# A diffusion backbone on one core: the last down projection turned to tokens on partitions, and a fourth buffer of rounded weights

## The chip, the cores and the metric

The kernel runs on one core of one Trainium2 chip. The metric is the device time of one execution in microseconds (us); the time before is the median of three runs, 1262.39 us (1262.36 to 1262.87). TensorE (PE) multiplies and writes to eight PSUM banks of 128 partitions x 512 fp32 values; VectorE (DVE), ScalarE (ACT) and GpSimd (POOL) work on SBUF, the first two also on PSUM; SyncE (SP) issues the loads of weights and the stores of the result.

## What the reference computes

Two layers over 256 latent and 256 context tokens of 1024 channels (P = 128, D = 1024, T = 512): layer 0 has attention, layer 1 a gated DeltaNet, and each ends with a SwiGLU part of hidden width 2816 = 22 x 128 (FT = 22). The change concerns the feed-forward part of layer 1 alone, where only the latent tokens are still needed:

```python
h = modulate(rms_norm(x, norm_g[l, 2]), sh2, sc2)
gate, up = jnp.split(h @ w_gate_up, 2, axis=-1)
y = (jax.nn.silu(gate) * up) @ w_down          # 256 x 2816 times 2816 x 1024
x = x + gt2 * (y * rsqrt(mean(y * y, axis=-1) + 1e-6)) * norm_g[l, 3]
```

`gt2` is a vector of 1024 channels, the same for all tokens; the output is `x` with tokens as rows.

## The kernel before

**Layout.** Activations lie with channels on partitions: `xT[:, k, token]` is channel tile k of 8. A channel's gate (`mods`) is then a value per partition, but a sum over channels, as the norm needs, is a matmul with a matrix of ones, and the output has to be transposed at the end.

**Products in parts.** Weights and activations are fp32 and are each split into a rounded part (fp32r, "hi") and the rest ("lo"). A product is hi x hi + lo x hi + hi x lo. SP loads weight chunks of up to 128 x 1024 values into eight slots `w_raw`; `split_to(n)` on ACT copies chunk n into one of three buffers `w_hi` (L1690), and `split_to(n)` on DVE subtracts that from the raw chunk in place, giving `w_lo` (L1918). ACT may write a `w_hi` buffer only when the products of the chunk three before are done, and `ahead(key)` lets it run two chunks ahead of the product being served.

**The feed-forward part of layer 1.** 44 gate and up chunks `("gate", 1, n)` of 8 contraction tiles, then 24 down chunks `("down", 1, m, part)` of 8, 8 and 6 tiles for each of the 8 output tiles m. `two()` (L1382 to L1394) issues two matmuls for each contraction tile: a weight hi tile is stationary and both parts of the activations move (512 columns, L1392 and L1393), then a weight lo tile and the activations' hi part (256 columns, L1391 and L1394). The first three gate chunks are multiplied together, tile by tile as `pre_norm(3)` delivers `h_both` (`project_lat_together`). Each result holds two halves that ACT copies and DVE adds. `act_both` holds the hidden values' two parts.

**The end.** `take_y` on ACT squares each output tile (L1746) and scales a copy by the gate (L1749), `sum_y` on DVE adds up the squares (L1991), `post_norm(3)` multiplies by ones (L1495), takes Ln and Exp (L1701, L1702), multiplies the 8 tiles by the factor and adds them to `xT` (L1998, L2002). TensorE then transposes `xT` in 16 blocks (L1665), DVE copies four banks of 512 to `out_sb` (L2157), and SP stores two rows of 128 tokens, 512 KB each (L2275).

**Before the feed-forward part.** `project_gdn_out`, `post_norm(2)` and `pre_norm(3)`: ones times the squares of `xT` (L1486), Ln, Exp, then for each channel tile DVE scales (L1958), ACT shifts and rounds (L1723, L1729), DVE takes the rest (L1971).

Each engine follows its own list in program order, held only by semaphores; `take(job, ring)` on TensorE takes the next bank of a ring and waits until its last content was read.

## Time and profile before

| | |
|---|---|
| median of three runs | 1262.39 us |
| profiled execution | 1263.51 us, its span 1261.8 us |
| busy | PE 1182.8 (94%), DVE 625.2, ACT 568.7, POOL 120.6 |
| mean granted TensorE clock | 0.974 |
| latest chain, share of span | PE 81%, DVE 9%, ACT 6% |
| feed-forward part of layer 1 | first matmul at 1053.06, down products from 1183.1 |
| after the last down matmul (starts 1245.09) | 16.7 us to the end of the span |

The span is counted from the first to the last instruction. A matmul's duration in the trace includes the way through the array, so in a dense stream the distance from start to start is the price, not the duration. A clock of 1.00 is 2.4 GHz, 0.50 is 1.2 GHz.

### The profile page before, as it was taken

The page shows a single profiled execution, that of the slowest core. Times are in us where ns is not written, and L with a number is a line of the kernel's source. Part 1 is how long each engine was busy: PE and PEld are TensorE (multiplying, and loading weights), DVE is VectorE, ACT ScalarE, POOL GpSimd, SP SyncE. Part 2 cuts the span into 40 slices and gives each one's busy share as a digit, 9 for nine tenths or more (in the row PEclk, how much of TensorE's full clock was granted, in tenths as well). Part 3 has the DMA queues.
Part 4 walks back from the last instruction along what each step waited for, and adds up shares of the span by engine and source line. Part 5 has one row for each costly group of instructions (what it writes and reads, how often), then busy time and mean ns, then how long its engine had stood idle before and what let it go on. Part 6 is the DMA issues. An engine that isn't in the chain of part 4 may idle for free.

```text
span 1261.8 us, 17880 instructions
## 1 busy us (share of the span) xinstructions
PE 1182.8 (94%) x7085; PEld 923.8 (73%) x7085; DVE 625.2 (50%) x1002; ACT 568.7 (45%) x1071; POOL 120.6 (10%) x116
## 2 busy tenths in 40 slices
PE   6899989989899999999999899999989997999996
PEld 3577734558378888888888558788779875888885
DVE  2532268652543332333222375589976525666554
ACT  2622246753462222223222376775355435665552
POOL 0030320110001111011000000010024100111000
PEclk9899999999999999999999999999979998999998
DMA  9655556642553333333333463234003042666560
GB/s 344 208 163 150 168 197 218 207 114 84 159 141 100 101 100 91 93 96 92 93 99 106 138 150 80 66 89 117 18 20 85 22 131 81 179 189 185 173 178 34
DMA packets 239390, 159.54 MB, mean 126 GB/s; under 512 B 14778, under 2 KB 213836, under 8 KB 239308
## 3 DMA queue, kind: packets, MB, share of 16 engines
q1 hardware_dynamic: 238528, 158.11, 42.5%
q8 instruction: 57, 0.93, 0.3%
q10 hardware_dynamic: 780, 0.29, 0.1%
q14 instruction: 25, 0.20, 0.1%
HBM read 157.33 MB, written 1.05 MB: 126 GB/s over the span
## 4 chain that ended last, share of the span: by engine, by line
PE 81%; DVE 9%; ACT 6%; issue 2%; DMA 1%; SPq 1%; POOL 0%; DVEq 0%; ACTq 0%; POOLq 0%
PE bank L1382 43%; PE bank L1393 9%; PE bank L1394 4%; PE bank L1369 2%; PE bank L1486 2%; PE bank L1436 2%; PE bank L1591 2%; PE bank L1467 1%; PE bank L1601 1%; DVE blocks L1020 1%; DVE outer L1018 1%; ACT h_work L1723 1%; PE bank L778 1%; PE bank L1622 1%; DMA w_raw<-in_ada_w 1%
## 5 line engine op out<-in xcount | busy, mean ns | idle before, releaser
L1382 PE MATMUL bank<-h_both,w_hi 128*128 128x512 f32 x1296 | 404.9, 394 | 2.5 <-issue 2.5
L1918 DVE TENSOR_TENSOR w_lo<-w_raw,w_hi 128x1024 fp32r<-128x1024 f32 (+1 forms) x179 | 220.5, 1234 | 244.3 <-ACT w_hi L1690 243.9
L1382 PEld LDWEIGHTS bank<-h_both,w_hi 128*128 128x128 f32 x1296 | 242.8, 188 | 53.7 <-issue 3.5
L1382 PE MATMUL bank<-h_both,w_lo 128*128 128x512 f32 x648 | 253.1, 391 | 0.0
L1690 ACT ACTIVATE w_hi<-w_raw 128x1024 fp32r<-128x1024 f32 (+1 forms) x179 | 184.0, 1031 | 72.5 <-PE bank L1382 52.9
L1382 PEld LDWEIGHTS bank<-h_both,w_lo 128*128 128x128 f32 x648 | 122.1, 188 | 25.9
L1393 PE MATMUL bank<-h_both,w_hi 128*128 128x512 f32 x308 | 113.0, 405 | 6.2 <-DVE h_both L1971 3.2
L1382 PE MATMUL bank<-act_both,w_hi 128*128 128x512 f32 x352 | 108.4, 389 | 0.0
L2176 POOL TENSOR_TENSOR act_both<-a_tmp,act_both 128x512 fp32r<-128x512 f32 (+1 forms) x44 | 44.7, 1016 | 466.1 <-ACT act_both L1792 283.9
L1394 PE MATMUL bank<-h_both,w_lo 128*128 128x256 f32 x308 | 87.5, 284 | 0.0
L1382 PEld LDWEIGHTS bank<-act_both,w_hi 128*128 128x128 f32 x352 | 66.1, 188 | 13.8
L1393 PEld LDWEIGHTS bank<-h_both,w_hi 128*128 128x128 f32 x308 | 59.3, 192 | 19.7 <-issue 7.1
L1382 PE MATMUL bank<-act_both,w_lo 128*128 128x512 f32 x176 | 68.5, 389 | 0.0
L1394 PEld LDWEIGHTS bank<-h_both,w_lo 128*128 128x128 f32 x308 | 59.4, 193 | 1.8
L1447 PE MATMUL bank<-h_whole,w_raw 128*128 128x256 f32 x256 | 59.1, 385 | 0.7 <-DVE h_whole L1074 0.7
L1393 PE MATMUL bank<-act_both,w_hi 128*128 128x512 f32 x168 | 59.7, 399 | 0.0
L1792 ACT ACTIVATE act_both<-a_tmp 128x512 fp32r<-128x512 f32 x22 | 13.9, 632 | 98.9 <-DVE a_tmp L2028 98.9
L1369 PE MATMUL bank<-w_raw,silu_pad 128*12 128x512 f32 (+2 forms) x384 | 53.0, 605 | 2.6 <-ACT silu_pad L1818 1.3
L1447 PEld LDWEIGHTS bank<-h_whole,w_raw 128*128 128x128 f32 x256 | 48.3, 193 | 7.4 <-issue 1.1
L1991 DVE TENSOR_TENSOR post_acc<-post_acc,post_sq 128x512 f32<-128x512 f32 (+1 forms) x28 | 15.6, 559 | 74.0 <-ACT y L1749 74.0
L1746 ACT ACTIVATE post_sq<-bank 128x512 f32<-128x512 f32 (+1 forms) x24 | 12.7, 527 | 87.5 <-PE bank L1382 67.4
L1857 ACT ACTIVATE probs<-bank,stats 128x256 f32<-128x256 f32 (+1 forms) x64 | 36.6, 579 | 31.0 <-DVE stats L2091 30.9
(283 smaller groups left out, 1693.0 us busy)
## 6 DMA issues: line engine op xcount, KB each, us to landing
w_raw<-in_ada_w SPq DMA_DIRECT2D x96, 512.0 KB, 5.0
w_raw<-in_ffn_w_gate_up SPq DMA_DIRECT2D x88, 512.0 KB, 3.8
w_raw<-in_ffn_w_down SPq DMA_DIRECT2D x32, 512.0 KB, 3.8
w_raw<-in_gdn_w_in SPq DMA_DIRECT2D x32, 512.0 KB, 4.0
w_raw<-in_attn_w_in SPq DMA_DIRECT2D x14, 512.0 KB, 3.9
w_raw<-in_ffn_w_down SPq DMA_DIRECT2D x16, 384.0 KB, 3.4
w_raw<-in_gdn_w_out SPq DMA_DIRECT2D x8, 512.0 KB, 5.2
w_raw<-in_attn_w_in SPq DMA_DIRECT2D x8, 256.0 KB, 3.5
```

The costliest lines, as they stand in the source:

```text
L1369: m = nc.tensor.matmul(banks[0][strip:strip + count, :], silu_pad[:, k, lead:lead + count], w[:, t, :], start=(group == 0 and k < ADA_STRIPS),
L1382: m = nc.tensor.matmul(dst, stationary(a, k), moving(b, k), start=(first and k == kk[0] and a == b == 0), stop=(last and k == kk[-1] and a ...
L1393: nc.tensor.matmul(halves, w(0, k), both, start=start, stop=False)
L1394: return nc.tensor.matmul(dst[:, 0:LAT], w(1, k), both[:, 0], start=False, stop=False)
L1436: m = nc.tensor.matmul(dst, w(a, k)[:, 0:width], (h_hi, h_lo)[b][:, k, lo:T], start=(k == a == b == 0), stop=(k == KT - 1 and a == 1))
L1447: m = nc.tensor.matmul(dst, raw_slot(key)[:, k, :], h_whole[:, k, :], start=(k == 0), stop=(k == KT - 1))
L1486: m = nc.tensor.matmul(dst[:, lo:T], ones, pre_sq[:, k % 4, lo:T], start=(k == 0), stop=(k == KT - 1))
L1591: finish(nc.tensor.matmul(dsts[m][:, 0:keys_of(qb)], q_sb[half, tile, qb * P:(qb + 1) * P], k_sb[half, key_tile(tile), 0:keys_of(qb)], sta ...
L1690: nc.scalar.activation(w_hi[m % N_SPLIT][:, 0:tiles, 0:w], raw_slot(key)[:, 0:tiles, 0:w], ACT.Copy).then_inc(w_hi_ready, 1)
L1857: release(nc.scalar.activation(probs[:, n % PROB_RING, m, 0:keys_of(qb)], bank(("s", n, m))[:, 0:keys_of(qb)], ACT.Exp, bias=stats[:, n % ...
L1918: nc.vector.tensor_tensor(w_lo[where[key] % N_RAW][:, 0:tiles, 0:w], raw_slot(key)[:, 0:tiles, 0:w], w_hi[m % N_SPLIT][:, 0:tiles, 0:w].bi ...
L2176: nc.gpsimd.tensor_tensor(act_lo[:, n // 2, lo:T], a_tmp[:, j % 2, lo:T], act_hi[:, n // 2, lo:T].bitcast(F32), ALU.subtract).then_inc(act ...
```

## The change

The down projection of layer 1 turns its operands round. Its weights are loaded as 22 chunks of two contraction tiles x 512 output channels (`LAST_HALVES`: half 0 or 1 of the channels, then c = 0 to 10). A hidden tile of 128 tokens is stationary (`late_hi`, `late_lo`, 128 x 128) and the weights move, 512 columns at a time, in three matmuls for each contraction tile and each of the two token tiles. The result `("z", half, t)` has tokens on partitions: ACT squares it and sums along the row in the same instruction, and the norm factor is a value per partition. The gate, now a vector along the row, is spread over the partitions by ones x a diagonal matrix that POOL makes (`gate_diag`), in two matmuls (`"row"` jobs). `xT` before the addition is transposed to tokens in four jobs `"xt"` of four blocks, the first before the feed-forward part and the others after gate chunks 10, 12 and 14; ACT copies all six banks to SBUF while it serves gates 4, 5, 6, 12, 14 and 16. DVE multiplies each z by the gate row, and when the factors are there makes each quarter of the output in one instruction, which SP stores as 256 KB.

In this feed-forward part `w_hi` has a fourth buffer, and ACT and DVE split three chunks ahead in place of two, so a buffer waits for the chunk four before it.

The core of the diff; left out are the places in memory, semaphores' names, the ring `"late"` of banks 0, 7 and 1, the removal of the i = 3 branches and of `post_norm(3)` on each engine, the same `hi_slot` and look-ahead in DVE's `split_to`, POOL's writing to `late_lo`, and the old down loop, which stays for layer 0:

```diff
+LAST_HALVES = [(half, c) for half in range(2) for c in range(FT // 2)]
+TOKENS = [(t, half) for t in range(LAT // P) for half in range(2)]
+TURNED_LATE = [("row", 0), ("row", 1), ("xt",) + TOKENS[0], ("xt",) + TOKENS[1], ("xt",) + TOKENS[2], ("xt",) + TOKENS[3]]
...
+    out += [("down", 1, half, c) for half, c in LAST_HALVES]
...
+        y_sums = stats[:, 0, 0:4].rearrange("p (h t) -> p h t", h=2)
+        y_rest, y_scale = stats[:, 1, 0:2], stats[:, 1, 2:4]
...
+        late_hi = at("late_hi", [FT, LAT], F32R, BIG)
+        late_lo = at("late_lo", [FT, LAT], F32R, BIG + FT * LAT * 4)
...
+        w_hi.append(at("w_hi_late", [KT, P], F32R, TAIL))
...
+        LATE = split_no[("gate", 1, 0)]
+        def hi_slot(n):
+            j = n - LATE
+            if j < 0:
+                return n % N_SPLIT
+            return (LATE + j % 4) % N_SPLIT if j % 4 < N_SPLIT else N_SPLIT
+        def hi_before(n):
+            return n - N_SPLIT if n < LATE + N_SPLIT else n - 4 if n > LATE + N_SPLIT else None
         def ahead(key, stop=None):
             last = len(split_chunks) - 1 if stop is None else split_no[stop]
-            return min(split_no[key] + 2, last)
+            return min(split_no[key] + (3 if split_no[key] > LATE else 2), last)
...
+                    if layer and n in LATE_AT:
+                        turn_late(TURNED_LATE[3 + LATE_AT.index(n)])
+                if layer:
+                    down_by_token()
+                    return
...
+            def turn_late(job):
+                dst = take(job, "late")
+                if job[0] == "row":
+                    pe.wait_ge(diag_ready, 1)
+                    m = nc.tensor.matmul(dst, ones, gate_diag[:, 4 * job[1]:4 * job[1] + 4, :], start=True, stop=True)
+                else:
+                    t, half = job[1:]
+                    pe.wait_ge(x_updated, 3 * KT)
+                    for k in range(4):
+                        m = nc.tensor.transpose(dst[:, k * P:(k + 1) * P],
+                                                xT[:, 4 * half + k, CTX + t * P:CTX + (t + 1) * P], ident)
+                finish(m, job)
+            def down_by_token():
+                for half in range(2):
+                    dsts = [take(("z", half, t)) for t in range(LAT // P)]
+                    def add(t, k, w, a, b):
+                        return nc.tensor.matmul(dsts[t], (late_hi, late_lo)[a][:, k, t * P:(t + 1) * P], w[b][:, k % 2, :],
+                                                start=(k == a == b == 0), stop=(k == FT - 1 and a == 1))
+                    for c in range(FT // 2):
+                        key = ("down", 1, half, c)
+                        w = [part.rearrange("p (t a) m -> p t (a m)", t=2) for part in weight_slots(key)]
+                        kk = (2 * c, 2 * c + 1)
+                        if half == 0:
+                            pe.wait_ge(act_hi_ready, FT + kk[1] + 1)
+                            pe.wait_ge(act_lo_ready, FT + kk[1] + 1)
+                        order = [(t, k) for k in kk for t in range(2)] if c < FT // 2 - 1 else [(t, k) for t in range(2) for k in kk]
+                        for t, k in order:
+                            for a, b in ((0, 0), (0, 1), (1, 0)):
+                                m = add(t, k, w, a, b)
+                            if k == FT - 1 and t == 0:
+                                finish(m, ("z", half, 0))
+                        finish(m, key)
+                    done_at[("z", half, 1)] = jobs[0]
...
+                for job in TURNED_LATE[:3]:
+                    turn_late(job)
                 ffn(1)
-                post_norm(3)
-            for half in range(2):
-                for t in range(LAT // P):
-                    dst = take(("out", t, half))
-                    for k in range(4):
-                        pe.wait_ge(x_updated, LAST_SUB * KT + 4 * half + k + 1)
-                        m = nc.tensor.transpose(dst[:, k * P:(k + 1) * P],
-                                                xT[:, 4 * half + k, CTX + t * P:CTX + (t + 1) * P], ident)
-                    finish(m, ("out", t, half))
...
-                    if m >= N_SPLIT:
-                        wait_product(act, split_job(split_chunks[m - N_SPLIT]))
+                    if m >= N_SPLIT and hi_before(m) is not None:
+                        wait_product(act, split_job(split_chunks[hi_before(m)]))
...
-                if i == 3:
-                    nc.scalar.activation(lat_sums[:, m % 2, 0:LAT], src[:, LAT:2 * LAT], ACT.Copy).then_inc(half_out, 1)
-                    wait_evacuated(act, ("y", i, m))
-                    src = lat_sums[:, m % 2]
...
-                if i == 3:
-                    last.then_inc(y_taken, 1)
-                else:
-                    release(last, ("y", i, m))
+                release(last, ("y", i, m))
...
-                    split_to(ahead(key))
+                    split_to(split_no[key] + 3 if layer else ahead(key))
...
-                            nc.scalar.activation(act_hi[:, n // 2, lo:T], a_tmp[:, j % 2, lo:T],
+                            nc.scalar.activation(late_hi[:, n // 2, :], a_tmp[:, j % 2, lo:T],
                                                  ACT.Copy).then_inc(act_hi_ready, 1)
+                        if n in COPIED_AT:
+                            job = TURNED_LATE[COPIED_AT.index(n)]
+                            wait_product(act, job)
+                            dst = gate_row if job[0] == "row" else x_tok[:, job[1], :]
+                            half = job[-1]
+                            release(nc.scalar.activation(dst[:, half * 512:(half + 1) * 512], bank(job), ACT.Copy), job)
...
+                if layer:
+                    square_by_token()
+                    return
...
+            def square_by_token():
+                for half, c in LAST_HALVES:
+                    split_to(ahead(("down", 1, half, c)))
+                    if c < FT // 2 - 1:
+                        continue
+                    for t in range(LAT // P):
+                        wait_product(act, ("z", half, t))
+                        nc.scalar.activation(s_tmp[:, t, :], bank(("z", half, t)), ACT.Square,
+                                             accum_out=y_sums[:, half, t:t + 1]).then_inc(y_squared, 1)
+                        if half:
+                            act.wait_ge(y_bias, 1)
+                            act.wait_ge(y_squared, 3 + t)
+                            link(nc.scalar.activation(y_scale[:, t:t + 1], y_sums[:, 1, t:t + 1], ACT.Ln,
+                                                      bias=y_rest[:, t:t + 1], scale=1.0 / D))
+                            nc.scalar.activation(y_scale[:, t:t + 1], y_scale[:, t:t + 1], ACT.Exp,
+                                                 scale=-0.5).then_inc(y_rstd, 1)
...
-                if i == 3:
-                    dve.wait_ge(half_out, 2 * FT + m + 1)
-                    release(nc.vector.tensor_tensor(lat_sums[:, m % 2, CTX:T], bank(("y", i, m))[:, 0:LAT],
-                                                    lat_sums[:, m % 2, 0:LAT], ALU.add), ("y", i, m))
-                    dve.wait_ge(y_taken, m + 1)
-                else:
-                    wait_evacuated(dve, ("y", i, m))
+                wait_evacuated(dve, ("y", i, m))
...
-                    split_to(ahead(("gate", layer, n)))
+                    split_to(split_no[("gate", layer, n)] + 3 if layer else ahead(("gate", layer, n)))
...
+                if layer:
+                    finish_by_token()
+                    return
...
+            def finish_by_token():
+                rows = lambda ap, half: ap[:, half * 512:(half + 1) * 512]
+                for half, c in LAST_HALVES:
+                    split_to(ahead(("down", 1, half, c)))
+                    if c < FT // 2 - 1:
+                        continue
+                    wait_evacuated(dve, ("row", half))
+                    for t in range(LAT // P):
+                        dve.wait_ge(y_squared, 2 * half + t + 1)
+                        nc.vector.tensor_tensor(rows(y_gated[:, t], half), bank(("z", half, t)), rows(gate_row, half),
+                                                ALU.mult).then_inc(y_gated_ready, 1)
+                    if half == 0:
+                        nc.vector.tensor_scalar(y_rest, y_sums[:, 0, :], 1.0 / D, RMS_EPS, ALU.mult,
+                                                ALU.add).then_inc(y_bias, 1)
+                dve.wait_ge(y_gated_ready, 4)
+                for t, half in TOKENS:
+                    wait_evacuated(dve, ("xt", t, half))
+                    dve.wait_ge(y_rstd, t + 1)
+                    nc.vector.scalar_tensor_tensor(out=rows(out_sb[:, t], half), in0=rows(y_gated[:, t], half),
+                                                   scalar=y_scale[:, t:t + 1], in1=rows(x_tok[:, t], half),
+                                                   op0=ALU.mult, op1=ALU.add).then_inc(out_ready, 1)
...
-                post_norm(3)
-            for half in range(2):
-                for t in range(LAT // P):
-                    job = ("out", t, half)
-                    wait_product(dve, job)
-                    release(nc.vector.tensor_copy(out_sb[:, t, half * 512:(half + 1) * 512], bank(job)), job)
...
+                wait_product(pool, ("y", 2, 0))
+                pool.wait_ge(mods_ready, 8)
+                nc.gpsimd.tensor_tensor(gate_diag, ident.unsqueeze(1).to_broadcast([P, KT, P]),
+                                        mods[:, 1, 5, :, 1:2].to_broadcast([P, KT, P]),
+                                        ALU.mult).then_inc(diag_ready, 1)
...
+                if kind == "down" and key[1]:
+                    return columns(ffn_w_down[1][2 * key[3] * P:2 * (key[3] + 1) * P, :], key[2] * 512, 512)
...
-            for t in range(LAT // P):
-                for half in range(2):
-                    wait_evacuated(sp, ("out", t, half))
-                sp.dma_start(out[0, t * P:(t + 1) * P, :], out_sb[:, t, :]).then_inc(out_stored, 16)
-            sp.wait_ge(out_stored, 16 * (LAT // P))
+            for n, (t, half) in enumerate(TOKENS):
+                sp.wait_ge(out_ready, n + 1)
+                cols = slice(half * 512, (half + 1) * 512)
+                sp.dma_start(out[0, t * P:(t + 1) * P, cols], out_sb[:, t, cols]).then_inc(out_stored, 16)
+            sp.wait_ge(out_stored, 16 * len(TOKENS))
...
+LATE_AT, COPIED_AT = (10, 12, 14), (4, 5, 6, 12, 14, 16)
```

## Rows read from the trace of the kernel before

**Rows 1.** Windows of 20 us: duration, busy (instructions) by engine, clock, DMA, GB/s.
```profile
1060.00:1080.00 20.00, 17.00 (x97) 14.46 (x96) 10.48 (x15) 12.22 (x21) 2.22 (x3) 1.00 0.56 157
...
1200.00:1220.00 20.00, 20.00 (x115) 17.38 (x114) 11.12 (x13) 10.49 (x16) 0.00 (x0) 1.00 0.65 190
```

**Rows 2.** Timeline, PE, around gate chunks 2 to 5: start, duration, what, idle before.
```profile
1063.94 0.39 PE L1392 MATMUL bank<-h_both,w_hi 128*128 128x512 f32 x1
1066.41 0.47 PE L1393 MATMUL bank<-h_both,w_hi 128*128 128x512 f32 x1 [2.08 <-DVE w_lo L1918]
...
1070.34 0.47 PE L1393 MATMUL bank<-h_both,w_hi 128*128 128x512 f32 x1 [0.92 <-DVE w_lo L1918]
...
1073.19 0.40 PE L1393 MATMUL bank<-h_both,w_hi 128*128 128x512 f32 x1
```

**Rows 3.** Timeline, ACT and DVE, the splits of chunks 3 and 4.
```profile
1063.95 1.05 ACT L1690 ACTIVATE w_hi<-w_raw 128x1024 fp32r<-128x1024 f32 x1
...
1067.89 1.04 ACT L1690 ACTIVATE w_hi<-w_raw 128x1024 fp32r<-128x1024 f32 x1
...
1065.04 1.23 DVE L1918 TENSOR_TENSOR w_lo<-w_raw,w_hi 128x1024 fp32r<-128x1024 f32 x1 [0.52 <-ACT w_hi L1690]
```

**Rows 4.** Timeline, PE, before the first gate products.
```profile
1044.19 5.71 PE L1486 MATMUL bank<-pre_sq,tab 128*128 128x256 f32 x16 [2.68 <-ACT pre_sq L1711]
1053.06 0.77 PE L1393 MATMUL bank<-h_both,w_hi 128*128 128x512 f32 x1 [3.16 <-DVE h_both L1971]
```

**Rows 5.** Windows of 1 us over the same place, columns as in rows 1.
```profile
1048.00:1049.00 1.00, 1.00 (x4) 0.79 (x4) 0.00 (x0) 0.40 (x2) 0.00 (x0) 0.64 0.00 0
...
1052.00:1053.00 1.00, 0.00 (x0) 0.00 (x0) 0.83 (x3) 0.97 (x4) 0.00 (x0) 0.57 0.00 0
...
1058.00:1059.00 1.00, 1.00 (x5) 0.81 (x5) 0.54 (x2) 0.05 (x1) 0.00 (x0) 0.52 0.00 0
```

**Rows 6.** Timeline, DVE, the second and the last two rests of `h_both`.
```profile
1053.78 0.42 DVE L1971 TENSOR_TENSOR h_both<-h_work,h_both 128x256 fp32r<-128x256 f32 x1 [0.53 <-ACT h_both L1729]
...
1057.78 0.76 DVE L1971 TENSOR_TENSOR h_both<-h_work,h_both 128x256 fp32r<-128x256 f32 x2 [0.37 <-ACT h_both L1729]
```

**Rows 7.** Timeline, PE: ones x 512 columns, and four transposes inside a dense stream.
```profile
193.25 1.02 PE L1639 MATMUL bank<-o_sq,tab 128*128 128x512 f32 x2
...
103.78 0.60 PE L1476 MATMUL bank<-tab,v_fm 128*128 128x128 f32 x4
104.13 0.71 PE L1382 MATMUL bank<-h_both,w_hi 128*128 128x512 f32 x2
```

**Rows 8.** Instructions on `act_both`: ns min/median/max, first and last start.
```profile
L1382 PE MATMUL bank<-act_both,w_hi x352: 389/389/390, 589.4 to 708.6; 128*128 128x512 f32 x176
L1382 PEld LDWEIGHTS bank<-act_both,w_lo x176: 187/188/188, 589.6 to 708.6; 128*128 128x128 f32 x176
...
L1393 PE MATMUL bank<-act_both,w_hi x168: 395/398/404, 1183.1 to 1244.6; 128*128 128x512 f32 x168
```

**Rows 9.** Timeline, ACT, DVE and SP, after the last down product.
```profile
1245.52 0.38 ACT L1741 ACTIVATE s_tmp<-bank 128x256 f32<-128x256 f32 x1 [5.34 <-PE bank L1392]
...
1254.78 2.47 DVE L2157 COPY out_sb<-bank 128x512 f32<-128x512 f32 x4
...
1256.75 0.95 SPq L2275 DMA_DIRECT2D out<-out_sb  x2
```

**Rows 10.** The two stores of `out_sb`: from issue to landing.
```profile
DMA to landing us min/median/max: 2.7/3.4/4.0
```

**Rows 11.** Groups by form: busy, mean ns | idle before: prices elsewhere in the kernel.
```profile
L1857 ACT ACTIVATION_READ_ACCUMULATOR probs<-bank,stats 128x1 f32 x64 | 12.8, 200 | 0.0
...
L1746 ACT ACTIVATE post_sq<-bank 128x512 f32<-128x512 f32 x16 | 9.6, 598 | 67.4 <-PE bank L1382 67.4
...
L2028 DVE TENSOR_TENSOR a_tmp<-bank,s_tmp 128x512 f32<-128x512 f32 x22 | 15.2, 691 | 55.3 <-PE bank L1382 55.3
...
L2131 DVE SCALAR_TENSOR_TENSOR o_sb<-o_sb,sub_gain,o_sq 128x512 f32<-128x512 f32 x4 | 3.0, 751 | 8.3 <-ACT o_sq L1702 8.3
```

57 lines of the change are left out of this document (28 added, 29 removed).

## The prediction

> **What bounds the kernel now.** I read the page first for the share of TensorE, then windows of 20 us over the last feed-forward part, then the places where TensorE waits in it, and last the chain from the last product to the end. From 1080 to 1240 every window has TensorE busy from end to end at a clock of 1.00, while DVE and ACT are busy little more than half of it and the DMA engines 0.65 [rows 1]. What is taken from another engine there is worth nothing; only fewer or faster matmuls count. Three places are not dense. Ahead of the first gate product TensorE has had nothing since 1044.19 + 5.71 = 1049.90 and starts at 1053.06 [rows 4], and its clock is at half from about 1052.14 to 1058.96: the window 1052 to 1053 has a mean of 0.57, so 0.14 us of it at full, and 1058 to 1059 has 0.52, so 0.04 us [rows 5]. Then gate chunks 3 and 4 come late [rows 2]. Last, from 1245.52, where ACT takes the last product up [rows 9], to 1261.8, the end of the span, 16.28 us pass with nothing beside them: the sum over tiles, the factor, 16 instructions on `xT`, the transposes, four copies, two stores.
>
> **The ends of the stalls: the fourth buffer.** The last matmul of the three first chunks starts at 1063.94 and takes its 0.23 in the stream, so the group ends at X = 1064.17. Chunk 3 starts at 1066.41 = X + 2.24, chunk 4 at 1070.34 = X + 6.17, chunk 5 at 1073.19 = X + 9.02 [rows 2]. The reason [rows 3]: the `w_hi` buffer of chunk 3 is free only when gate 0 is done, then come 1.05 us on ACT and 1.23 us on DVE; chunk 4 has its turn on ACT at 1067.89, after the table load and the activation of the first pair. With four buffers chunk 3 is split during `pre_norm(3)`, when ACT has just finished and TensorE is busy with the group. The two later turns of ACT and DVE stay, but each serves one chunk more: chunk 4 is ready at X + 2.24 and needed at X + 2.82 (8 tiles x 0.353), chunk 5 is ready at X + 6.17 and needed at X + 5.64, a rest of 0.53. So chunk 5 starts at X + 6.17 in place of X + 9.02: **-2.85**. I walked ACT's queue on with its extra copies (six of 512 columns at about 0.6 [rows 11]) and found chunk 7 ready 0.9 before it is needed and chunk 9, after two of the copies, 0.95 before; so they cost nothing. The cover is thin: a lag of 1 us more on ACT at gates 4 to 6 would show as a stall of the same size, and at worst the whole 2.85 come back.
>
> **The jobs ahead of the first gate.** Two ones-products of 512 columns (1.02 each with its way out) and four transposes (0.35 to the next start, and the following record reads 0.71) [rows 7] make 2 x 1.0 + 0.45 = 2.45 us; they can begin at 1049.90 and end at 1052.35, before 1053.06 [rows 4]. The diagonal comes from POOL, which has from the first output tile of the mixer on to do it and nothing else. Without this gap they would cost 2.45. They do something more: they fill the idle after which the clock fell. If it stays at full, the group of three chunks takes 3 x 0.35 = 1.05 us for a channel tile and is held by TensorE, not by `h_both`: its second tile is ready at 1053.78 + 0.42 = 1054.20 and its last at 1058.54, 0.8 apart on average [rows 6]. Seven tiles from 1054.3 end at 1061.6, against 1064.17: **-2.6**. If it falls all the same, 0. I take the full value, since the clock held through the dense stretches and after each fall there had been an idle of 2 us or more [rows 4, 5]; both ends stay in the range.
>
> **The three later `xt` jobs** stand in the dense stream: 3 x 0.45 = **+1.35** (0.35 to 0.60 each [rows 7], so 1.05 to 1.8). Their banks were read long before; nothing waits for them but copies.
>
> **The down products.** Columns are the same: 176 x 768 = 264 x 512 = 135,168. Before, 174 pairs take from 1183.1 to 1244.6, 0.3534 each, so 176 take 62.2 us [rows 8]. After, 264 matmuls of 512 columns. Layer 0 has that form, three matmuls for a tile: 526 starts in 589.4 to 708.6, 0.2266 each [rows 8], which gives 59.8. By columns alone, 0.3534 x 512/768 = 0.2356, it would be 62.2. The form speaks for the first, and the loads, twice as dense here [rows 1], for a little more: 0.2285, 60.3 us, **-1.9** (0 to -2.4). A weight load of 188 ns lies under each matmul there as it would here. The splits cost 1.05 on ACT and 1.23 on DVE for 2.74 us of products [rows 3], and the loads are of the same bytes in longer rows, so neither binds. The squares of half 0 lie beside the products of half 1.
>
> The Trainium skill, TensorE: Matmul & The Clock Gate, section "Wait — 56ns, not 53.3ns?", gives a warm matmul N / 2.4 GHz plus a fixed 2.5 ns or so. By it 176 pairs take 57.2 us and 264 wide ones 57.0, so turning the operands would give 0.2 and not 1.9, and the whole change -13.2. The trace has 226.6 ns for 512 columns against the page's 215.8, so its floor is too small here.
>
> **After the last product.** Let T be the moment when ACT takes up the last product, 1245.52 before [rows 9]. The square takes 0.60 and the read of the accumulator 0.20, with a small overlap 0.76. ACT has done token tile 0 by then: its product ended six matmuls = 1.4 us earlier, and square, read, Ln and Exp of one column take about that. Ln and Exp of tile 1 lie beside DVE's multiplication of 0.69, which ends at T + 1.5. Then four instructions of 0.75 [rows 11], starts 0.08 closer than that as in the four copies (2.47 for four of 0.68 [rows 9]): 2.75, T + 4.3. Before, the last copy ended at 1254.78 + 2.47 = 1257.25, and the span 4.55 later, with 1 MB of stores nearly all still ahead; the first landed 2.7 after its issue, the second 4.0 [rows 10]. The landings are 1.85 apart for 512 KB, so a quarter of 256 KB moves in up to 0.9, one is issued every 0.67, and three are nearly through when the last starts. I take 3.1 from the last result to the end of the span (2.6, if it is a 2.7 shortened by half its bytes with 0.55 around it, to 4.55, as now). T + 7.4 against T + 16.28: **-8.9** (-7.4 to -9.4).
>
> **Sum.** -2.6 - 2.85 + 1.35 - 1.9 - 8.9 = -14.9. The span goes from 1261.8 to 1246.9, the profiled execution's time of 1263.51 to 1248.6. The median of the runs shown, 1262.39, is 1.1 below the profiled execution, so the forecast is 1247.5.
>
> **Rivals.**
> 1. *The clock falls all the same* before the first gate, or rises late. For it: the jobs end near 1052.35 and a gap of 0.7 follows, four of the six instructions are transposes, and TensorE worked at half clock at 1048 even while busy [rows 5]. Against it: 1.9 us of ones-products, the kind of work during which the clock rose at about 1048.72 [rows 5]. +2.6, 1250.1. The Trainium skill says on the same page, Part 4, that transposes do not count as busy for the clock; by that the ones-products alone would have to hold it.
> 2. *The wait moves*: ACT, with six more copies and a later first activation, delivers a chunk late at gates 4 to 9, and the fourth buffer gives nothing. Up to +2.85, 1250.4. Against it the margins of 0.9 worked out above.
> 3. *Slower than before*: the weight load of the activations no longer lies under the matmul, because the stationary tile alternates between two token tiles and two banks. Exposed whole it is 264 x 0.188 = 49.6 us [rows 8], 1297. It decides from 14.9 / 264 = 0.056 us more for a matmul, that is a pace of 0.285. Against it layer 0, which changes its stationary tile as often.
> 4. *No change to be measured*: the tail must keep its length, so the stores or the factor must cost some 9 us more than worked out. A store takes at most 4.0 [rows 10], so hardly anything is left for it.
>
> **Chances and range.** Forecast 0.70, rival 1 0.19, rival 2 0.08, rival 3 0.02, rival 4 0.01. The forecast's own bounds: down products 59.8 to 62.2, tail -9.4 to -7.4, transposes 1.05 to 1.8, together 1246.2 to 1251.3 if all fall on one side. Rivals 1 and 2 reach to 1250.4, or 1252 with a middling tail. To hold 8 in 10 I give 1244.5 to 1251.8, the lower end for gains that I have not seen, such as the rest of 0.53. 0.2% of 1262.4, 2.5 us, is about what a measurement of this kernel can tell from no change. Faster by more than that 0.97, within it 0.01, slower 0.02.
>
> **What the profile after would show.** The clock in 1052 to 1059 at 1.00, or not: that parts forecast and rival 1. One wait of TensorE for `w_lo` of about 0.5 after chunk 4, not two of 3.0 together. 264 matmuls 0.228 apart, some 60.3 us. Between the last product and the end of the span 7.4 us, of it one read of the accumulator, 0.69 and four times 0.75 on DVE. The prediction would be wrong if TensorE waited in the gates for ACT, if the pace were 0.235 or more, or if the last quarter's store took as long as one of 512 KB behind another.

## The result and the profile after

The changed kernel takes 1246.82 us (median of 4 runs, 1245.89 to 1247.54), the kernel before, run beside it, 1262.38 (1261.07 to 1262.87): a ratio of 0.9877 with a 95% interval of 0.9862 to 0.9893, or 15.6 us less. The forecast was 1247.5, range 1244.5 to 1251.8. One execution of run 1 below took 6598.31 us for a cause that nothing here shows, and stands in no ratio.

The profiled execution of the changed kernel took 1245.89 us, its span 1244.3. That is 17.5 less than the span of before, so 2 us more than the medians differ. These 2 us lie in front of all that was changed: the first gate of layer 1 starts at 1051.00 against 1053.06 [rows 4]. Most of them are one fall of the clock in layer 0, which this execution of the kernel before had and this one of the changed kernel had not: TensorE's rows of the two lie 0.5 us apart at 280 and 2.1 apart four us later. Run 1, which has the same program there as the kernel before, reads 1.00 in this window too, so the fall belongs to the execution and not to the change. The same window in both, first before, then after:

```profile
280.00:285.00 5.00, 4.97 (x15) 3.99 (x16) 0.00 (x0) 0.00 (x0) 0.00 (x0) 0.66 0.01 3
```
```profile
280.00:285.00 5.00, 5.00 (x23) 4.10 (x23) 0.00 (x0) 0.00 (x0) 0.00 (x0) 1.00 0.02 3
```

Over all fourteen profiles of this study the first gate of layer 1 starts between 1050.5 and 1053.7, whatever was changed behind it. So I compare stretches counted from there. The change's windows of 20 us (columns as in [rows 1]):

```profile
1060.00:1080.00 20.00, 19.58 (x112) 16.90 (x111) 12.59 (x19) 14.74 (x27) 2.88 (x4) 1.00 0.85 229
...
1200.00:1220.00 20.00, 20.00 (x90) 16.47 (x89) 10.59 (x11) 8.87 (x12) 0.00 (x0) 1.00 0.63 185
```

The first had 17.00 of TensorE [rows 1] and has 19.58; of the stalls 0.42 is left. TensorE's timeline from the last gap to chunk 5 (beside [rows 2, 4]):

```profile
1042.12 5.71 PE L1515 MATMUL bank<-pre_sq,tab 128*128 128x256 f32 x16 [2.68 <-ACT pre_sq L1771]
1047.67 1.88 PE L1573 MATMUL bank<-gate_diag,tab 128*128 128x512 f32 x4
1049.39 0.60 PE L1578 MATMUL bank<-tab,xT 128*128 128x128 f32 x4
1051.00 0.47 PE L1418 MATMUL bank<-h_both,w_hi 128*128 128x512 f32 x1 [1.01 <-DVE h_both L2050]
...
1059.48 0.39 PE L1417 MATMUL bank<-h_both,w_hi 128*128 128x512 f32 x1
1059.71 0.39 PE L1418 MATMUL bank<-h_both,w_hi_late 128*128 128x512 f32 x1
...
1065.89 0.47 PE L1418 MATMUL bank<-h_both,w_hi 128*128 128x512 f32 x1 [0.42 <-DVE w_lo L1997]
```

The three jobs fill the gap, chunk 3 (in `w_hi_late`) follows the first three without a pause, and chunk 5 is 0.42 late. The clock, in the same place as [rows 5] (window of 1 us, the third number from the end):

```profile
1046.00:1047.00 1.00, 1.00 (x4) 0.78 (x4) 0.00 (x0) 0.33 (x1) 0.00 (x0) 0.67 0.00 0
1047.00:1048.00 1.00, 1.00 (x5) 0.76 (x4) 0.00 (x0) 0.13 (x1) 0.00 (x0) 1.00 0.00 0
...
1050.00:1051.00 1.00, 0.00 (x1) 0.03 (x1) 0.83 (x3) 1.00 (x3) 0.00 (x0) 1.00 0.00 0
1051.00:1052.00 1.00, 1.00 (x5) 0.88 (x6) 0.47 (x2) 1.00 (x3) 0.00 (x0) 1.00 0.00 0
```

It is full from 1047 on and every window of the gates reads 1.00. The down products by tile (beside [rows 8]), then TensorE, ACT, DVE and SP's queue at the end by their timelines (beside [rows 9, 10]), and the landings of the four stores:

```profile
L1588 PE MATMUL bank<-w_hi,late_hi x68: 389/389/397, 1177.0 to 1236.6; 128*128 128x512 f32 x68
```
```profile
1237.01 0.39 PE L1588 MATMUL bank<-w_hi,late_lo 128*128 128x512 f32 x1
...
1236.57 0.19 ACT L1869 ACTIVATION_READ_ACCUMULATOR s_tmp<-bank 128x1 f32 x1
1236.86 0.30 ACT L1874 ACTIVATE stats<-stats 128x1 f32<-128x1 f32 x1
1237.19 0.20 ACT L1876 ACTIVATE stats<-stats 128x1 f32<-128x1 f32 x1
1237.44 0.60 ACT L1869 ACTIVATE s_tmp<-bank 128x512 f32<-128x512 f32 x1
...
1236.87 0.69 DVE L2121 TENSOR_TENSOR y_gated<-bank,gate_row 128x512 f32<-128x512 f32 x1 [8.06 <-ACT s_tmp L1869]
1238.16 0.69 DVE L2121 TENSOR_TENSOR y_gated<-bank,gate_row 128x512 f32<-128x512 f32 x1 [0.60 <-ACT s_tmp L1869]
1238.89 2.74 DVE L2130 SCALAR_TENSOR_TENSOR out_sb<-y_gated,stats,x_tok 128x512 f32<-128x512 f32 x4
...
1239.67 2.32 SPq L2375 DMA_DIRECT2D out<-out_sb  x4
```
```profile
DMA to landing us min/median/max: 2.1/2.1/2.1
```

264 products take from 1177.04 to 1237.24, 60.20 us or 0.2280 each. From the end of the last product to the end of the span there are 7.06 us, before 16.48 (1245.33 to 1261.8).

**The stretches of all fourteen profiles**, in us. "Group" is from the first gate product to the end of the first three chunks, which I call X as in the prediction; "to chunk 5" from X to chunk 5; "gates" from there to the first down product; "down" from that to the end of the last; "end" from that to the end of the span. Each is a difference of two rows of TensorE's timeline, the end of a dense matmul being its start + 0.235 (0.12 for 256 columns). For run 3, in which a ones-product stands between chunks 4 and 5, "to chunk 5" holds that product too.

| kernel | group | to chunk 5 | gates | down | end | sum |
|---|---|---|---|---|---|---|
| before | 11.12 | 9.02 | 109.95 | 62.18 | 16.48 | 208.74 |
| changed | 8.71 | 6.18 | 111.15 | 60.20 | 7.06 | 193.30 |
| 1 buffer alone | 11.13 | 6.16 | 110.00 | 61.85 | 16.42 | 205.57 |
| 2 three buffers | 8.73 | 9.06 | 111.27 | 60.19 | 7.13 | 196.38 |
| 3 gap empty | 11.19 | 6.17 | 112.66 | 60.20 | 7.12 | 197.34 |
| 4 ones in the gap | 8.73 | 9.06 | 109.98 | 62.03 | 16.40 | 206.21 |
| 5 transposes in the gap | 8.73 | 9.06 | 109.94 | 62.19 | 16.47 | 206.39 |
| 6 narrow | 8.72 | 6.18 | 111.15 | 63.06 | 7.06 | 196.17 |
| 7 two stores | 8.72 | 6.17 | 111.30 | 60.21 | 7.51 | 193.91 |
| 8 end early | 8.73 | 6.15 | 111.09 | 60.21 | 6.29 | 192.48 |
| 9 table early | 8.71 | 5.69 | 111.10 | 60.21 | 7.12 | 192.85 |
| 10 all three | 8.73 | 5.70 | 110.40 | 60.21 | 6.26 | 191.30 |
| 11 before, narrow | 11.05 | 9.08 | 109.94 | 63.35 | 16.44 | 209.86 |
| 12 short rows | 8.72 | 6.16 | 111.31 | 60.20 | 6.93 | 193.32 |

A stretch that an edit does not touch repeats to about 0.1 us, the gates with the jobs in them and the changed end to 0.2, the down products of before to 0.3. Each ratio below is to the kernel before as it ran beside that run, whose medians lie between 1262.16 and 1262.98. The medians of two different runs therefore compare to about 1 us only, and what is smaller is read from the stretches.

### The profile page after: what moved, and what is told of

It reads as the page before. It is cut to its first block, busy times and chain, and to the rows that moved or that the text cites. A ratio compares the mean times of both kernels' runs of the same rounds, so it can differ in the third digit from the quotient of the medians.

```text
span 1244.3 us, 17650 instructions
## 1 busy us (share of the span) xinstructions
PE 1174.4 (94%) x6999; PEld 914.8 (74%) x6999; DVE 617.3 (50%) x973; ACT 564.2 (45%) x1061; POOL 122.5 (10%) x117
## 3 DMA queue, kind: packets, MB, share of 16 engines
HBM read 157.33 MB, written 1.05 MB: 127 GB/s over the span
## 4 chain that ended last, share of the span: by engine, by line
PE 80%; DVE 8%; ACT 7%; issue 2%; DMA 1%; SPq 1%; POOL 0%; DVEq 0%; ACTq 0%; POOLq 0%
PE bank L1407 43%; PE bank L1418 6%; PE bank L1588 5%; PE bank L1419 3%; PE bank L1394 2%; PE bank L1515 2%; PE bank L1658 2%; ACT h_work L1783 2%; PE bank L1496 1%; PE bank L1668 1%; DVE blocks L1045 1%; DVE outer L1043 1%; PE bank L803 1%; PE bank L1465 1%; DMA w_raw<-in_ada_w 1%
## 5 line engine op out<-in xcount | busy, mean ns | idle before, releaser
L1407 PE MATMUL bank<-h_both,w_hi 128*128 128x512 f32 x1296 | 403.7, 393 | 2.5 <-issue 2.5
L1997 DVE TENSOR_TENSOR w_lo<-w_raw,w_hi 128x1024 fp32r<-128x1024 f32 (+1 forms) x161 | 200.8, 1249 | 229.7 <-ACT w_hi L1750 228.7
L1407 PEld LDWEIGHTS bank<-h_both,w_hi 128*128 128x128 f32 x1296 | 242.1, 188 | 53.4 <-issue 3.5
L1750 ACT ACTIVATE w_hi<-w_raw 128x1024 fp32r<-128x1024 f32 (+1 forms) x161 | 167.0, 1040 | 76.9 <-PE bank L1407 52.9
L1418 PE MATMUL bank<-h_both,w_hi 128*128 128x512 f32 x231 | 83.0, 398 | 1.4 <-DVE h_both L2050 1.0
L1407 PE MATMUL bank<-act_hi,w_hi 128*128 128x512 f32 x176 | 68.5, 389 | 0.0
L1407 PE MATMUL bank<-act_lo,w_hi 128*128 128x512 f32 x176 | 68.5, 389 | 0.0
L1407 PE MATMUL bank<-act_hi,w_lo 128*128 128x512 f32 x176 | 68.5, 389 | 0.0
L1851 ACT ACTIVATE act_hi<-a_tmp 128x512 fp32r<-128x512 f32 x22 | 13.9, 632 | 98.9 <-DVE a_tmp L2101 98.9
L2270 POOL TENSOR_TENSOR act_lo<-a_tmp,act_hi 128x512 fp32r<-128x512 f32 x22 | 28.5, 1294 | 282.3 <-ACT act_hi L1851 282.3
L1418 PEld LDWEIGHTS bank<-h_both,w_hi 128*128 128x128 f32 x231 | 43.4, 188 | 11.2 <-issue 1.9
L1465 PE MATMUL bank<-h_both,w_hi 128*128 128x512 f32 (+1 forms) x96 | 33.3, 431 | 10.7 <-DVE h_both L2050 10.7
```

The lines of the kernel that those rows point to most:

```text
L1407: m = nc.tensor.matmul(dst, stationary(a, k), moving(b, k), start=(first and k == kk[0] and a == b == 0), stop=(last and k == kk[-1] and a ...
L1418: nc.tensor.matmul(halves, w(0, k), both, start=start, stop=False)
L1465: m = nc.tensor.matmul(dst, w(a, k)[:, 0:width], (h_hi, h_lo)[b][:, k, lo:T], start=(k == a == b == 0), stop=(k == KT - 1 and a == 1))
L1750: nc.scalar.activation(w_hi[hi_slot(m)][:, 0:tiles, 0:w], raw_slot(key)[:, 0:tiles, 0:w], ACT.Copy).then_inc(w_hi_ready, 1)
L1997: nc.vector.tensor_tensor(w_lo[where[key] % N_RAW][:, 0:tiles, 0:w], raw_slot(key)[:, 0:tiles, 0:w], w_hi[hi_slot(m)][:, 0:tiles, 0:w].bit ...
L2270: nc.gpsimd.tensor_tensor(low, a_tmp[:, j % 2, lo:T], hi.bitcast(F32), ALU.subtract).then_inc(act_lo_ready, 1)
```

## The experiments

Theory: the change is five separate terms, each where the prediction put it. Rivals: the waits only move, the clock held by chance, the pace of the down products has another cause than the number of matmuls, the end is set by the stores.

**1. The fourth buffer alone**, on the kernel before: `hi_slot`, `hi_before` and the look-ahead of the change, and

```diff
+        w_hi.append(at("w_hi_late", [KT, P], F32R, TAIL))
...
-                    split_to(ahead(key))
+                    split_to(split_no[key] + 3 if layer else ahead(key))
```

> The kernel before with the fourth buffer of rounded weights and the look-ahead of three chunks in the last feed-forward part, and nothing else of the change. My theory (each late turn of ACT and DVE serves one chunk more): the two waits of TensorE for w_lo, 2.1 and 0.9 us, give way to one of about 0.5, chunk 5 starts 6.2 us after the end of the first three chunks in place of 9.0, and the time is 2.85 us below the kernel before, 1259.5. Rival (ACT's list is the limit and the wait only moves): two waits with the same sum and 1262.4. Second rival (the buffer matters only together with the filled gap): less than 1 us.

Measured: 1259.46 us, ratio 0.9969 (0.9958 to 0.9981), so 2.4 to 5.3 us less; by stretches 2.86 from X to chunk 5. The view of waits for TensorE in the gates (us, times, longest):

```profile
PE bank L1407 <- DVE h_both L1985: 3.2, 1, 3.2
...
PE bank L1407 <- DVE w_lo L1932: 0.4, 1, 0.4
```

3.0 us in two waits became 0.4 in one, with the gap and the slow clock still there. The term stands by itself.

**2. Three buffers in the changed kernel**: `hi_slot` returns n % 3, `hi_before` n - 3, and the look-ahead is 2.

> The changed kernel with three buffers and a look-ahead of two as before, all else as changed. My theory: the waits for w_lo of 2.1 and 0.9 us are back behind the first three chunks, nothing else moves, 2.4 to 2.9 us above the changed kernel, 1249.2 to 1249.7. Rival (the down products by token, with 2.7 us of products for each chunk and longer copies on ACT in the gates, need the fourth buffer throughout): TensorE waits again and again in gates 4 to 9 or in the down products, and the time is 5 us or more above the changed kernel.

Measured: 1250.15 us (0.9882 to 0.9915). That is 3.3 above the changed kernel by the medians, 2.65 by the two ratios (0.9898 and 0.9877) and 3.08 by the stretches, a little more than my 2.4 to 2.9; 2.88 of it lies between X and chunk 5, and 0.12 in the gates, 0 in the down products. All of TensorE's waits for `w_lo` are these two, by the view of waits:

```profile
PE bank L1415 <- DVE w_lo L1994: 2.9, 2, 2.1
```

So the fourth buffer is worth 2.9 at one place, in both kernels, and nothing in the rest of the part.

**3. The gap left empty**:

```diff
-                for job in TURNED_LATE[:3]:
-                    turn_late(job)
...
-LATE_AT, COPIED_AT = (10, 12, 14), (4, 5, 6, 12, 14, 16)
+LATE_AT, COPIED_AT = (4, 6, 8, 12, 14, 16), (6, 8, 10, 14, 16, 18)
```

> The changed kernel with the two ones-products and the first group of transposes moved from the gap before the first gate to the dense stream, after gates 4, 6 and 8 (the other three after 12, 14 and 16). My theory: the gap of 3.2 us is idle again, the clock is at half for some 6 us of the first gates, +2.4, and the three jobs cost their 2 x 0.95 + 0.45 = 2.35 us in the stream: 4.75 above the changed kernel, 1251.6. Rival (the clock held in the changed execution by chance, not by the jobs): the granted clock stays at 1.00 over the first gates and only +2.35 remains, 1249.2.

Measured: 1250.1 us (0.9885 to 0.9915), 3.3 above the changed kernel; by stretches 4.0. The idle is back and with it the half clock, first in TensorE's timeline (with the first ones-product in its new place), then in two windows of the group:

```profile
1050.86 0.76 PE L1418 MATMUL bank<-h_both,w_hi 128*128 128x512 f32 x1 [3.16 <-DVE h_both L2048]
...
1067.62 1.02 PE L1573 MATMUL bank<-gate_diag,tab 128*128 128x512 f32 x2
1068.22 0.64 PE L1418 MATMUL bank<-h_both,w_hi 128*128 128x512 f32 x1
```
```profile
1052.00:1053.00 1.00, 1.00 (x5) 0.84 (x4) 0.96 (x4) 1.00 (x4) 0.00 (x0) 0.50 0.00 0
1056.00:1057.00 1.00, 1.00 (x6) 0.86 (x5) 0.51 (x3) 0.80 (x1) 0.00 (x0) 0.62 0.00 0
```

The group takes 11.19, +2.48. The three jobs in the stream cost only +1.50 (6.17 + 112.66 against 6.18 + 111.15) and not 2.35. Two things fit that: the first ones-product, at X + 5.57, stands mostly where TensorE waits for chunk 5 anyway (chunk 5 starts at X + 6.17 here and at X + 6.18 in the changed kernel), and a ones-product takes 0.86 from start to start (two in 1047.67 to 1049.39 there) and not 0.95. By its time alone the run decides nothing, since 1250.1 lies nearer to the rival's 1249.2 than to my 1251.6; the rows of the clock and the group's 2.48 exclude the rival.

**4. Two ones-products in the gap of the kernel before**, results unread:

```diff
+            def fill_gap():
+                pe.wait_ge(x_updated, 3 * KT)
+                for n in range(2):
+                    nc.tensor.matmul(banks[0], ones, xT[:, n, :], start=True, stop=True)
...
+                fill_gap()
                 ffn(1)
```

> The kernel before with two ones-products of 512 fp32 columns in the gap before the first gate of layer 1, whose results nobody reads: TensorE works there 1.9 us more, and nothing else differs. My theory: the clock stays at full over the first gates and the time falls by about 2.4 us to 1260.0, by adding work alone. Rival (the gain at this place came from another cause than the filled gap, or 1.9 us are too little to hold it): the clock falls near the start of the gates as in the kernel before, and the time is 1262.4.

Measured: 1259.87 us, ratio 0.9979 (0.9970 to 0.9989), so 1.4 to 3.8 us less, from work added. TensorE's timeline with the fill and the gap that is left, and a window in the group:

```profile
1048.56 1.88 PE L1502 MATMUL bank<-xT,tab 128*128 128x512 f32 x4
1051.89 0.47 PE L1393 MATMUL bank<-h_both,w_hi 128*128 128x512 f32 x1 [1.45 <-DVE h_both L1978]
```
```profile
1052.00:1053.00 1.00, 1.00 (x6) 0.77 (x6) 0.47 (x3) 1.00 (x4) 0.00 (x0) 1.00 0.06 16
```

The group takes 8.73 as in the changed kernel, -2.39, and nothing else moved but by the noise. What was won there is the clock, not the jobs' removal from elsewhere.

**5. Twenty transposes in the same gap**:

```diff
...
+                for n in range(20):
+                    k = n % KT
+                    nc.tensor.transpose(banks[0][:, n % 4 * P:(n % 4 + 1) * P], xT[:, k, CTX:CTX + P], ident)
```

> The kernel before with twenty transposes of 128 x 128 fp32 blocks in the gap before the first gate of layer 1, whose results nobody reads, some 2.0 us of work on TensorE. Theory A (any work of TensorE holds the clock): clock 1.00 over the first gates and about 2.4 us less, 1260.0. Theory B (the Trainium skill, TensorE: Matmul & The Clock Gate, Part 4: transposes do not count as busy): the clock falls as in the kernel before, 1262.4. The twin with ones-products tells how far the gap matters at all.

Measured: 1260.32 us, ratio 0.9979 (0.9969 to 0.9988), and a group of 8.73. Theory B is refuted for these fp32 transposes. TensorE's timeline, and two windows of 1 us:

```profile
1050.28 2.35 PE L1503 MATMUL bank<-tab,xT 128*128 128x128 f32 x20
1053.61 0.47 PE L1393 MATMUL bank<-h_both,w_hi 128*128 128x512 f32 x1 [0.98 <-DVE h_both L1979]
```
```profile
1053.00:1054.00 1.00, 0.39 (x2) 0.38 (x3) 0.76 (x2) 1.00 (x4) 0.00 (x0) 1.00 0.00 0
1056.00:1057.00 1.00, 1.00 (x8) 0.86 (x7) 0.96 (x3) 1.00 (x3) 0.00 (x0) 1.00 0.00 0
```

**6. The down products in halves of 256 columns**, in the changed kernel:

```diff
-                        return nc.tensor.matmul(dsts[t], (late_hi, late_lo)[a][:, k, t * P:(t + 1) * P], w[b][:, k % 2, :],
...
+                        for side in range(2):
+                            cols = slice(256 * side, 256 * (side + 1))
+                            m = nc.tensor.matmul(dsts[t][:, cols], (late_hi, late_lo)[a][:, k, t * P:(t + 1) * P], w[b][:, k % 2, cols],
...
+                        return m
```

> The changed kernel with each down matmul of 512 columns as two of 256 with the same stationary tile: 528 matmuls in place of 264, the same columns, each with a weight load of its own. Theory A (a matmul costs its columns at 2.4 GHz and a fixed 14 to 15 ns, which is why 88 matmuls fewer saved 2.0 us): 528 x (106.7 + 15) ns = 64.2 us of down products in place of 60.2. Theory B (the pairs before were held by the weight load beside the 256-column matmul, which takes 188 ns in the trace and overlaps only in part): much more than 64, up to 528 x 188 ns = 99 us. Theory C (the floor of 2.5 ns of the Trainium skill, TensorE: Matmul & The Clock Gate, is all that comes with a matmul, and the rest of the pace is contention in proportion to columns): 61.5 us.

Measured: one execution, span 1248.2, time 1251.2 (3.0 above its span, where the other kernels have 1.5 to 1.8, so the time is not used). The last products and one of the tile rows:

```profile
1240.90 0.40 PE L1590 MATMUL bank<-w_hi,late_lo 128*128 128x256 f32 x2
```
```profile
L1590 PE MATMUL bank<-w_lo,late_hi x176: 274/283/283, 1178.3 to 1240.8; 128*128 128x256 f32 x176
```

The first of these rows holds two matmuls, so the last starts at 1241.02 and the down products take 63.06 us, 119.4 ns each. The expectation for run 11 was still worked out from 62.94, 119.2 and 10.4, which count to the first of the two. Neither A (64.2) nor B; C gave 61.5, and its own rule, 2.5 ns for each of 264 matmuls more, makes that 60.9, further off still. A matmul more costs (63.06 - 60.20) / 264 = 10.8 ns. The weight load reads 187 to 192 ns here, but products follow each other 119 ns apart, so loads overlap. TensorE's loading is busy without a break, though (PEld, the second of the busy times; its records overlap):

```profile
1200.00:1220.00 20.00, 20.00 (x170) 20.00 (x169) 9.92 (x11) 8.67 (x11) 0.00 (x0) 1.00 0.60 184
```

so part of the 10.8 ns may be the load itself; this run does not tell them apart. If a matmul costs at other widths what it costs here, the 88 matmuls fewer are worth 0.95 of the 1.98 us won.

**11. The kernel before with three matmuls of 256** for its pair:

```diff
...
-                                last = two(dst, lambda p, k: w(p, k - a), act_both[:, :, k, CTX:T], k, k == 0, k == FT - 1)
+                                both = act_both[:, :, k, CTX:T]
+                                first, final = k == 0, k == FT - 1
+                                nc.tensor.matmul(dst[:, 0:LAT], w(0, k - a), both[:, 0], start=first, stop=False)
+                                nc.tensor.matmul(dst[:, LAT:2 * LAT], w(0, k - a), both[:, 1], start=False, stop=False)
+                                last = nc.tensor.matmul(dst[:, 0:LAT], w(1, k - a), both[:, 0], start=False, stop=final)
```

> The kernel before, whose 512-column down matmul over the two strided parts of the activations is made as two of 256 columns with the same stationary weights: three matmuls of 256 for a pair, 528 in all, as many and as wide as in the narrow form of the changed kernel. Open is what the rest of the 2.0 us is: there a matmul more cost 10.4 ns, so 88 fewer explain 0.9. Theory A (the moving operand in two parts 2 KB apart costs the rest): 528 come out as in the narrow form, 119.2 ns each, 62.9 us, 0.7 more than the pairs' 62.2 though 176 matmuls more would cost 1.8. Theory B (the weights as stationary operand, the other roles, or the loads of short rows slow each column): each costs some 2 ns more, 64.0 us.

Measured: 63.35 us, 120.0 ns each: between A (62.9) and B (64.0). The last tile row of it:

```profile
L1537 PE MATMUL bank<-act_both,w_lo x176: 278/283/283, 1180.9 to 1243.8; 128*128 128x256 f32 x176
```

With the same number and width of matmuls the two role assignments differ by 0.29 (63.35 against 63.06), no more than the down products of before vary from one execution to the next (61.85 to 62.19). With 10.8 ns for each of 176 fewer, the pairs of before should take 61.4 and take 62.18, 0.7 more, which would be the price of the wide matmul that moves two parts. The three parts, 0.95, 0.29 and 0.74, add up to the whole term by the way they are formed, so their sum proves nothing, and runs 6 and 11 are one execution each. Shown is that narrow matmuls cost more in both kernels (+2.86 and +1.17 us); the split of the 1.98 between number, roles and moving pattern is a working out, not shown.

**12. Down weights loaded in rows of 512 B**, in the changed kernel:

```diff
...
+                        for g in range(4):
+                            cols = slice(P * g, P * (g + 1))
+                            sp.dma_start(dst[:, :, cols], src[:, :, cols]).then_inc(done, 16)
```

> The changed kernel with each down chunk of two tiles x 512 channels loaded by four DMAs of 128 channels, so in rows of 512 B as before in place of 2 KB; the products are untouched. Theory A (the row length of loads that run beside the products does not slow TensorE): down products 60.2 us as in the changed kernel. Theory B (short rows take more of the memory's time and the rest of the 2.0 us came from the longer rows): about 61.3 us. In both the loads land long before they are needed.

Measured: one execution, 1245.66 us; down products 60.20, as in the changed kernel. The longer rows of the loads gave nothing.

**7. The result in two stores of 512 KB**:

```diff
-                sp.wait_ge(out_ready, n + 1)
-                sp.dma_start(out[0, t * P:(t + 1) * P, cols], out_sb[:, t, cols]).then_inc(out_stored, 16)
+                sp.wait_ge(out_ready, 2 * t + 2)
+                sp.dma_start(out[0, t * P:(t + 1) * P, :], out_sb[:, t, :]).then_inc(out_stored, 16)
```

> The changed kernel with the result stored as two DMAs of 512 KB as before, each when both its quarters are there, in place of four of 256 KB. My theory (a store takes some 1.45 us and then 0.65 us for 256 KB): the last store starts when its second quarter is ready and takes 2.7 in place of 2.1, 0.6 to 0.7 us more from the last result to the end, 1247.5. Rival (four issues cost as much as they save): no difference, 1246.8.

Measured: 1247.37 us (0.9863 to 0.9893), end 7.51 against 7.06 (6.93 to 7.13 in the other runs that leave the end as it is), so some +0.4. The landings of its stores:

```profile
DMA to landing us min/median/max: 2.7/2.7/2.7
```

A store lands 2.7 after its issue, not 2.1, and from the last result to the end there are 3.13 us, not 2.67. The theory holds with a smaller size; what gives back the rest of the 0.6 is not shown.

**8. One output made early**: DVE makes the first quarter between its two multiplications.

```diff
                         nc.vector.tensor_tensor(rows(y_gated[:, t], half), bank(("z", half, t)), rows(gate_row, half),
...
+                        if half and t == 0:
+                            put_out(0, 0)
```

> The changed kernel with one output instruction of DVE moved forward: the first quarter of the output is made between the two multiplications of the second half, where DVE waits 0.6 us for ACT's square. My theory (DVE's list sets the end: multiplication and four outputs of 0.67): the last quarter is ready 0.6 us earlier, 1246.2, if the factor of token tile 0 is there when the multiplication of tile 0 ends, as it is by 0.2 us. Rival (the factor of tile 1 from ACT then comes last, or the stores are the limit): less than 0.3 us.

Measured: 1246.5 us (0.9856 to 0.9885), end 6.29, -0.77. DVE's timeline has no idle between the first multiplication and the last output:

```profile
1237.69 0.75 DVE L2119 SCALAR_TENSOR_TENSOR out_sb<-y_gated,stats,x_tok 128x512 f32<-128x512 f32 x1
1238.36 0.68 DVE L2130 TENSOR_TENSOR y_gated<-bank,gate_row 128x512 f32<-128x512 f32 x1
1238.96 2.07 DVE L2119 SCALAR_TENSOR_TENSOR out_sb<-y_gated,stats,x_tok 128x512 f32<-128x512 f32 x3
```

From the last result to the end of the span there are 2.67 us as in the changed kernel. So DVE's list sets the end, and the stores follow it.

**9. The activation table early**: `preload_act_table_set` on ACT after the split of chunk 3.

> The changed kernel with ACT's table for the activation loaded right after the split of chunk 3, where ACT waits 2.3 us for the first product, and not at the first activation. My theory (the table load of 1.28 us stands in the chain that makes chunk 5 late): TensorE's last wait for w_lo in the gates, 0.42 us, is gone, 1246.4. Rival (chunk 5 is held by the order of the copies alone): the wait stays.

Measured: chunk 5 at X + 5.69, no wait of TensorE for `w_lo` in the gates, -0.49. The load in its new place, by ACT's timeline, ends before ACT takes up the first product at 1060.67:

```profile
1058.41 1.28 ACT L1826 ACT_TABLE_LOAD   x1
```

It takes 1.28 us and moving it wins 0.49, nearly all that there was to win: in a dense stream chunk 5 would start at X + 5.64. The median of the time is 1247.17 (0.9866 to 0.9899): 0.4 us can't be seen in it.

**10. All three**: runs 8 and 9, and five of the six jobs in the gap, the two more in the banks of gates 3 and 4.

```diff
-                for job in TURNED_LATE[:3]:
+                for job in TURNED_LATE[:5]:
```

> The changed kernel with three things: the output's first quarter made early by DVE, the activation table loaded in ACT's wait for the first product, and five of the six jobs of ones and transposes in the gap before the first gate, where TensorE is idle for another 1.0 us (two of them in banks that the later gates need; ACT copies them in its wait). My theory: 0.6 + 0.42 + 2 x 0.45 = 1.9 us below the changed kernel, 1244.9. Rival (the two copies on ACT delay the copy of gate 0 or a bank holds gate 3): 1246 or more, with a new wait of TensorE behind the first three chunks.

Measured: 1245.14 us, ratio 0.9865 (0.9850 to 0.9880); by stretches 191.30, 2.0 below the changed kernel (-0.48 to chunk 5, -0.75 in the gates, -0.80 at the end). The two more groups of transposes end just as the first gate can start, and no wait came in their place. TensorE's timeline:

```profile
1049.99 1.47 PE L1578 MATMUL bank<-tab,xT 128*128 128x128 f32 x12
1051.60 0.47 PE L1418 MATMUL bank<-h_both,w_hi 128*128 128x512 f32 x1
```

Its median is the lowest of all, 1.7 below the changed kernel, though the intervals of the two ratios overlap.

## Why the prediction was right

| term | forecast | measured, by stretches | runs that show it |
|---|---|---|---|
| clock over the first three chunks | -2.6 | -2.41 | 3, 4, 5 |
| fourth buffer | -2.85 | -2.84 | 1, 2 |
| three `xt` jobs in the stream | +1.35 | +1.20 | 10 |
| down products | -1.9 | -1.98 | 6, 11, 12 (the cause in part) |
| end | -8.9 | -9.42 | 7, 8 |
| sum | -14.9 | -15.44 | |

**The clock.** The forecast took it that filling the gap holds the clock; rival 1 had 0.19. In the windows of 1 us it reads 1.00 over the whole group in all ten profiles in which the gap was filled, and 0.50 over most of it in the four in which it was empty: before, runs 1, 3 and 11. That it was the filling was not shown by the changed kernel, since the jobs came with it; run 4, where nothing but the fill was added, shows it, and run 3 from the other side. The 0.2 that is missing is the pace of the group. Its second tile starts 1.20 after the first:

```profile
1052.20 0.50 PE L1418 MATMUL bank<-h_both,w_hi 128*128 128x512 f32 x1
```

That is no later than the 1.24 of the sum, but the seven tiles from there to X take 7.51 us, 1.07 each, and not 1.05. The rests of `h_both` come 0.72 apart on average by the numbers that the prediction gives, not 0.8; that changes nothing, since TensorE takes longer for a tile.

**The fourth buffer.** Step by step as worked out: chunk 3 at X, chunk 4 at X + 2.81, chunk 5 at X + 6.18 for a forecast of X + 6.17. The walk along ACT's queue with its extra copies was right too: rival 2 would have shown as a wait in the gates, and the stretch has only the transposes' 1.20 more.

**The `xt` jobs** cost 0.40 each and not 0.45 (1.20 for three; run 10, which takes two of them away, gains 0.75). The three jobs in the gap take 2.32 us (1047.67 to 1049.99) for a forecast of 2.45, and fit with 1.01 to spare.

**The down products.** The size was right and its reason only half: the pace was read from layer 0's form, 0.2266, with a little added, and came out as 0.2280. The reason behind it, that a matmul has a fixed price so that fewer wide ones are better, would explain 0.95 of 1.98, if the price of run 6 holds at 512 columns; what the rest is stays open. The Trainium skill's fixed cost (TensorE: Matmul & The Clock Gate, "Wait — 56ns, not 53.3ns?") would have given 0.2. That figure is for matmuls one behind the other; where each has a weight load of its own, the trace does not agree with it: 10.8 ns for a matmul with its load (run 6) against 2.5.

**The end** was mis-sized by 0.5. The multiplication ended 1.41 after ACT took the last product up (1.5 forecast) and the four outputs took 2.74 (2.75). The store term was the one: from the last result, 1238.89 + 2.74 = 1241.63, to the end of the span 2.67 and not 3.1. I had spaced landings 0.9 apart, from 1.85 for 512 KB; they keep up with the issues 0.67 apart, and each takes 2.1. The lower bound, 2.6, was the right reading.

**The rivals that fell.** A weight load that is exposed (rival 3) is out: even 256-column matmuls follow each other at 119 ns. That the median came out 0.7 below the forecast is the sum of these sizes, -0.5, and the runs' spread.

## What to carry to other kernels

When a tuned kernel waits, ask what the idle does beyond its own length: here 3.2 us of idle cost 2.4 us more by the clock behind it, and unread work in the gap was already a gain. Put work that has to be done anyway into the gap in front of a dense stretch, as long as it ends before the stretch can start. A buffer more was worth 2.85 us at the one place where ACT's and DVE's turns come late, and nothing in the steady part; and where the norm factor is wanted per row of the output, getting rows on partitions turns a sum by matmul, a scaling, a transpose and a copy into one instruction for each bank.

## What the runs showed of the hardware

- fp32 transposes on TensorE held the clock at 1.00 as well as products with ones did (run 5: 2.35 us of them, group 8.73; run 4: 1.88 us of products, 8.73; empty: 11.12). The Trainium skill, TensorE: Matmul & The Clock Gate, Part 4, says that transposes do not count as busy in the same way and that the full clock does not engage for them; run 5, the one test of it here, does not agree for fp32 blocks. It shows that they kept a full clock, not that they would raise a low one.
- In run 3, with 3.16 us of idle ahead of the first gate product at 1050.86, the clock was still at half five microseconds later (0.50 to 1056, then 0.62); after 0.98, 1.01 and 1.45 us of idle, behind filled gaps (run 5, the changed kernel, run 4), it stayed at 1.00.
- A 256-column fp32r matmul with its own 128 x 128 weight load follows the one before after 119 ns, though the load reads 187 to 192 ns in the trace; 512 columns after 228 ns.
- Loads in rows of 512 B or of 2 KB made no difference to products running beside them: 60.20 us in both.
